# Dilated attention: the table for the exchange of weights is made one unit earlier on VectorE

## The chip, the cores and the metric

The kernel runs on one core of a Trainium2 chip. The core has five engines that work beside each other: TensorE (PE in the profile; PEld is its loading of weights), VectorE (DVE), ScalarE (ACT), GpSimd (POOL) and SyncE (SP), which issues the transfers. Each engine takes its instructions in the order written; engines wait for each other by semaphores. The metric is the device time of one execution in microseconds (us); less is better.

## The reference, cut to what matters

The program computes three transformer layers over 512 tokens of width 1024. The second layer is a dilated attention with 8 heads of width 128 in three groups (windows 128, 512 and 2048, dilations 1, 4 and 16). Each group has its own queries; keys and values are shared.

```python
def _dilated_mixer(x, w_in, w_out, pos):
    z = x @ w_in
    ...
    for g, (span, dilation) in enumerate(DIL_PAIRS):
        o, l = _dilated_window_branch(q[:, g], k, v, span, dilation)   # softmax within a band; l is its log-sum-exp
        outs.append(o)
        lses.append(l)
    wts = jax.nn.softmax(jnp.stack(lses, axis=0), axis=0).astype(v.dtype)
    o = jnp.einsum('gbht,gbhtd->bhtd', wts, jnp.stack(outs, axis=0))
```

So every token of every head needs the log-sum-exp of all the groups before the weighted probabilities can be formed. In the kernel the first group has its tokens in order of time, the others in order of their residue modulo 4; the log-sum-exps have to change places between the two orders. This is the exchange.

## The kernel before, in words

The projection `z = x @ w_in` and the attention run together. The projection is cut into 40 **units** (class `Product`, tag `c_`), five for each head: three of queries (r = 0, 1, 2), one of keys (r = 3), one of values (r = 4). A unit is 24 matmuls of 128x512 on TensorE (lines 954 to 956: high weights with high and low inputs, low weights with high inputs, for 8 tiles k).

`Chain` writes the order of each engine out by hand. For unit j:

- TensorE (`Chain.pe`): the 24 matmuls; between the fourth and the fifth tile k the attention's `middle(j)`; after the last its `pe(j)`.
- ScalarE (`Chain.act`): waits until TensorE has used unit j, makes the high half of the weights of the unit four ahead (L853), copies the unit's result out of its bank (L2206), then the attention's `act(j)`.
- VectorE (`Chain.dve`): the same wait, the low half of these weights (L860, which waits for L853), the rotation of queries or keys (L2218 to L2223, not for r = 4), then the attention's `dve(j)`.

The attention (class `Dilated`) does its steps by their distance `rel` from the unit in which the values of head h are projected: `heads_at(j, (rel,))` gives the head for which unit j has this distance. The steps of one head around the change:

- rel 0 to 3: TensorE `score` (L2291, L2292, L2297, L2298) behind the unit, VectorE the row maxima (L2428 to L2431), ScalarE the exponentials (L2409) with their sums. Behind the exponentials of rel 3 ScalarE takes the logarithm of the sums (L2414, semaphore `logged`).
- rel 4: VectorE waits for `logged`, subtracts the negated maxima (L2435), spreads the eight numbers of a row over the table `flat` of 128x256 (L2440, semaphore `spread`) and adds two parts of the probabilities (L2443, semaphore `summed`). TensorE turns the values of head h behind the unit (`values`, L2310), ScalarE copies them out (L2392).
- rel 5, in the middle of the unit: TensorE waits for `spread` and does the `exchange` (L2320, L2321), then the second turn of the values (L2310), which needs the bank that ScalarE emptied with L2392. After the unit ScalarE and VectorE make the factors (L2448, L2380, L2450, L2452) and scale the probabilities (L2455 to L2459).
- rel 6 to 9: the probabilities are turned (L2330) and multiplied with the values (L2343, L2349); VectorE finishes a head with L2462 at rel 9.

Rel 5 of head h is rel 0 of head h + 1: behind the middle of that unit stands the first `score` of the next head, which waits for the rotation of its keys (L2223, done by VectorE at rel 4 of head h).

For the last head rel 1 to 9 fall behind the projection, among the matmuls of the output projection (L983, L984, L991); there VectorE has nothing between the steps of rel 3 and rel 4.

Of the kernel before, what the change touches and what calls it, by code (L numbers as in the profile page):

```python
# [273 lines left out]
class Evac:  # L274
# [8 lines left out]
    def start(self, dve):  # L283
        pass
# [4 lines left out]
    def dve(self, dve, core, b, i):  # L289
        pass  # L290
# [12 lines left out]
class Scaled(Evac):  # L303
# [5 lines left out]
    def dve(self, dve, core, b, i):  # L309
        dve.wait_ge(self.rms.late.inv, 2)  # L310
        dve.scalar_tensor_tensor(self.Z[:, b + self.off, :], core.bank(i), self.scale, core.line[INV2][:],
                                 ALU.mult, ALU.mult).then_inc(core.freed(i), 1)
# [1913 lines left out]
class Dilated:  # L2226
# [192 lines left out]
    def dve(self, dve, j):  # L2419
        core, s = self.core, self.s  # L2420
        for h, r in self.heads_at(j, (0, 1, 2, 3)):
            bank = core.psum[(3, 7)[r % 2]]
            negmax = self.stat(h, "negmax")
            dve.wait_ge(s.scored, 4 * h + r + 1)
            if h >= 2 and r == 0:
                dve.wait_ge(s.turned, 3 * h - 3)
            if r == 0:
                dve.tensor_reduce(negmax[:, 0:1], bank[:, 0:P], AX.X, ALU.max, negate=True).then_inc(s.negmax, 1)  # L2428
                dve.tensor_reduce(negmax[:, 1:2], bank[:, 2 * P:4 * P], AX.X, ALU.max, negate=True).then_inc(s.negmax, 1)
            else:  # L2430
                dve.tensor_reduce(negmax[:, 2 * r:2 * r + 2], bank.rearrange("p (e k) -> p e k", e=2), AX.X, ALU.max, negate=True).then_inc(s.negmax, 1)  # L2431
        for h, _ in self.heads_at(j, (4,)):
            negmax, lse = (self.stat(h, n) for n in ("negmax", "lse"))
            dve.wait_ge(s.logged, h + 1)
            dve.tensor_tensor(lse, lse, negmax, ALU.subtract).then_inc(s.lse, 1)  # L2435
            dve.wait_ge(s.lse, h + 1)
            if h:
                dve.wait_ge(s.exchanged, h)
            eye = core.const("eye32").rearrange("p (o i) -> p o i", o=1).broadcast_to([P, 8, 32])
            dve.tensor_tensor(self.flat.rearrange("p (g i) -> p g i", i=32), lse.rearrange("p (g o) -> p g o", o=1).broadcast_to([P, 8, 32]),  # L2440
                              eye, ALU.mult).then_inc(s.spread, 1)
            res = self.res[h % 2].rearrange("p (c g k) -> p c g k", c=4, g=2)
            dve.tensor_tensor(res[:, :, 0, :], res[:, :, 0, :], res[:, :, 1, :], ALU.add).then_inc(s.summed, 1)  # L2443
        for h, _ in self.heads_at(j, (5,)):
            negmax, sums, other, factor = (self.stat(h, n) for n in ("negmax", "sum", "other", "factor"))
            band, res = self.band[h % 2], self.res[h % 2].rearrange("p (c g k) -> p c g k", c=4, g=2)
            dve.wait_ge(s.exchanged, h + 1)
            dve.tensor_tensor(other, core.psum[4][:, 0:8], negmax, ALU.add).then_inc(s.shifted, 1)  # L2448
            dve.wait_ge(s.other, h + 1)
            dve.tensor_tensor(other, other, sums, ALU.add).then_inc(s.total, 1)  # L2450
            dve.wait_ge(s.total, h + 1)
            dve.reciprocal(factor, other).then_inc(s.inverted, 1)  # L2452
            dve.wait_ge(s.inverted, h + 1)
            by = lambda a, b, n: factor[:, a:b].rearrange("p (g o) -> p g o", o=1).broadcast_to([P, b - a, n])
            dve.tensor_scalar(band[:, 0:P], band[:, 0:P], factor[:, 0:1], None, ALU.mult).then_inc(s.scaled, 1)  # L2455
            wide = band[:, P:7 * P].rearrange("p (g k) -> p g k", g=3)
            dve.tensor_tensor(wide, wide, by(1, 4, 2 * P), ALU.mult).then_inc(s.scaled, 1)
            dve.wait_ge(s.summed, h + 1)
            dve.tensor_tensor(res[:, :, 0, :], res[:, :, 0, :], by(4, 8, P), ALU.mult).then_inc(s.scaled, 1)  # L2459
        for h, _ in self.heads_at(j, (9,)):  # L2460
            dve.wait_ge(s.src_hi, h + 1)
            dve.tensor_tensor(self.in_time(self.xl[:, h, :]), self.result(), self.in_time(self.xh[:, h, :].bitcast(F32)),  # L2462
                              ALU.subtract).then_inc(s.src_lo, 1)
# [698 lines left out]
```

## Time and profile before

| | before |
|---|---|
| median of 3 runs | 2458.71 us (2455.76 to 2458.79) |
| the profiled execution, its own time | 2457.42 us |
| its span in the trace | 2455.6 us |
| granted TensorE clock, mean over the span | 0.941 |
| TensorE busy | 2206.9 us (90%) |
| VectorE busy | 1252.5 us (51%) |
| ScalarE busy | 842.3 us (34%) |

The dilated attention with its projection lies between about 900 and 1225 us. In the timeline a line is: start in us, duration in us, engine, line of the program, operation, out<-in, shape and count; in square brackets how long the engine had been idle before it and what released it. The durations of matmuls overlap, since they are pipelined; their pace is read from start to start. A granted clock of 1.00 is TensorE's upper level (2.4 GHz), one of 0.50 the lower (1.2 GHz).

### The profile page before, as it was taken

The page shows a single profiled execution, that of the slowest core. Times are in us where ns is not written, and L with a number is a line of the kernel's source. Part 1 is how long each engine was busy: PE and PEld are TensorE (multiplying, and loading weights), DVE is VectorE, ACT ScalarE, POOL GpSimd, SP SyncE. Part 2 cuts the span into 40 slices and gives each one's busy share as a digit, 9 for nine tenths or more (in the row PEclk, how much of TensorE's full clock was granted, in tenths as well). Part 3 has the DMA queues.
Part 4 walks back from the last instruction along what each step waited for, and adds up shares of the span by engine and source line. Part 5 has one row for each costly group of instructions (what it writes and reads, how often), then busy time and mean ns, then how long its engine had stood idle before and what let it go on. Part 6 is the DMA issues. An engine that isn't in the chain of part 4 may idle for free. (4 is left out here: it accounts for less than half of the span.)

```text
span 2455.6 us, 31441 instructions
## 1 busy us (share of the span) xinstructions
PE 2206.9 (90%) x12852; PEld 1740.7 (71%) x12852; DVE 1252.5 (51%) x1663; ACT 842.3 (34%) x1304; POOL 317.9 (13%) x302
## 2 busy tenths in 40 slices
PE   8996787899999978999989999989996668999997
PEld 6863784678887867777768788876664446878875
DVE  4644761663243366565464443466576535542543
ACT  3334322353232243434343322352224234322322
POOL 0000000200000210000030690052341103000002
PEclk9997897899999989999989999999998779999999
DMA  5210000222222212121123223222110011323222
GB/s 201 95 43 14 2 4 1 95 86 90 99 95 86 95 61 69 61 69 61 35 69 112 90 95 100 97 86 94 52 44 5 1 69 61 119 73 116 95 76 70
DMA packets 50607, 177.16 MB, mean 72 GB/s; under 512 B 5616, under 2 KB 5616, under 8 KB 50208
## 3 DMA queue, kind: packets, MB, share of 16 engines
q1 hardware_dynamic: 46944, 164.65, 20.4%
q10 hardware_dynamic: 3168, 7.60, 0.8%
q0 software_dynamic: 352, 2.90, 0.3%
q8 instruction: 102, 1.67, 0.3%
q14 instruction: 41, 0.34, 0.0%
HBM read 170.94 MB, written 4.19 MB: 71 GB/s over the span
## 5 line engine op out<-in xcount | busy, mean ns | idle before, releaser
L860 DVE TENSOR_TENSOR w_lo<-w_raw,w_hi 128x1024 fp32r<-128x1024 f32 (+1 forms) x320 | 396.1, 1239 | 838.2 <-ACT w_hi L853 837.0
L954 PE MATMUL banks<-xh,w_hi 128*128 128x512 f32 x1560 | 626.1, 401 | 4.0 <-PEq L213 3.6
L853 ACT ACTIVATE w_hi<-w_raw 128x1024 fp32r<-128x1024 f32 (+1 forms) x320 | 329.0, 1031 | 863.4 <-PE banks L956 806.5
L956 PE MATMUL banks<-xh,w_lo 128*128 128x512 f32 x1560 | 615.0, 394 | 0.0
L955 PE MATMUL banks<-xl,w_hi 128*128 128x512 f32 x1560 | 614.5, 394 | 0.0
L954 PEld LDWEIGHTS banks<-xh,w_hi 128*128 128x128 f32 x1560 | 297.6, 191 | 83.4 <-issue 16.4
L956 PEld LDWEIGHTS banks<-xh,w_lo 128*128 128x128 f32 x1560 | 296.9, 190 | 63.9
L955 PEld LDWEIGHTS banks<-xl,w_hi 128*128 128x128 f32 x1560 | 298.0, 191 | 60.4 <-issue 0.7
L954 PE MATMUL banks<-hh,w_hi 128*128 128x512 f32 x688 | 270.6, 393 | 11.8 <-DVE w_lo L860 4.8
L956 PE MATMUL banks<-hh,w_lo 128*128 128x512 f32 x688 | 269.2, 391 | 0.0
L955 PE MATMUL banks<-hl,w_hi 128*128 128x512 f32 x688 | 269.2, 391 | 0.0
L954 PEld LDWEIGHTS banks<-hh,w_hi 128*128 128x128 f32 x688 | 130.1, 189 | 41.1 <-issue 7.3
L955 PEld LDWEIGHTS banks<-hl,w_hi 128*128 128x128 f32 x688 | 130.2, 189 | 27.4 <-issue 0.5
L956 PEld LDWEIGHTS banks<-hh,w_lo 128*128 128x128 f32 x688 | 130.0, 189 | 27.4
L590 POOL TENSOR_TENSOR line<-Y 128x512 f32<-128x512 f32 x4 | 5.2, 1294 | 1046.2 <-DVE Y L573 1046.2
L983 PE MATMUL banks<-xh,w_hi 128*128 128x512 f32 x168 | 77.1, 459 | 66.3 <-DVE w_lo L860 34.1
L983 PEld LDWEIGHTS banks<-xh,w_hi 128*128 128x128 f32 x168 | 37.1, 221 | 84.2 <-DVE w_lo L860 38.6
L984 PE MATMUL banks<-xh,w_lo 128*128 128x512 f32 x168 | 74.3, 442 | 0.0
L991 PE MATMUL banks<-xl,w_hi 128*128 128x512 f32 x168 | 54.6, 429 | 1.9 <-DVE xl L727 1.9
L701 POOL TENSOR_TENSOR line<-line,line 128x512 f32<-128x512 f32 x2 | 2.6, 1288 | 406.4 <-ACT line L694 406.4
L368 DVE TENSOR_TENSOR line<-line 128x512 f32<-128x512 f32 x64 | 48.5, 757 | 0.0
L371 DVE TENSOR_TENSOR hl<-line,hh 128x512 fp32r<-128x512 f32 x64 | 47.2, 737 | 2.2
(502 smaller groups left out, 2869.9 us busy)
## 6 DMA issues: line engine op xcount, KB each, us to landing
w_raw<-in_w SPq DMA_DIRECT2D x128, 512.0 KB, 3.5
w_raw<-in_w_gu SPq DMA_DIRECT2D x44, 512.0 KB, 3.5
w_raw<-in_w_c_in SPq DMA_DIRECT2D x40, 512.0 KB, 3.4
w_raw<-in_w_ab_in SPq DMA_DIRECT2D x27, 512.0 KB, 3.5
w_raw<-in_w_in SPq DMA_DIRECT2D x25, 512.0 KB, 3.5
w_raw<-in_w_down SPq DMA_DIRECT2D x16, 384.0 KB, 3.1
w_raw<-in_w_down SPq DMA_DIRECT2D x16, 320.0 KB, 2.8
w_raw<-in_w_ab_out SPq DMA_DIRECT2D x8, 512.0 KB, 3.5
```

Of the source, the lines that this page charges most:

```text
L368: dve.tensor_tensor(sq[:], relu[:], relu[:], ALU.mult).then_inc(self.s.squared, 1)
L371: dve.tensor_tensor(self.hl[:, b, :], sq[:], self.hh[:, b, :].bitcast(F32), ALU.subtract).then_inc(self.s.hidden_lo, 1)
L590: done(gp, gp.tensor_tensor(line[SUM][:], Y[:, 0, :], Y[:, 1, :], ALU.add), s.sum)
L701: done(gp, gp.tensor_tensor(line[SSUM][:], line[SQ0][:], line[SQ1][:], ALU.add), s.ssum)
L853: act.activation(core.w_hi[u % SLOTS][:, 0:n], core.raw[u % RAW][:, 0:n], ACT.Copy).then_inc(core.hi_ready, 1)
L860: dve.tensor_tensor(lo[:, 0:n], core.raw[u % RAW][:, 0:n], hi[:, 0:n].bitcast(F32), ALU.subtract).then_inc(core.split_ready, 1)
L954: pe.matmul(bank, hi[:, w], src.xh[:, kk, :], start=kk == 0, stop=False)
L955: pe.matmul(bank, hi[:, w], src.xl[:, kk, :], start=False, stop=False)
L956: mm = pe.matmul(bank, lo[:, w], src.xh[:, kk, :], start=False, stop=last)
L983: pe.matmul(banks[i], hi[:, w], src.xh[:, k, :], start=k == 0, stop=False)
L984: pe.matmul(banks[i], lo[:, w], src.xh[:, k, :], start=False, stop=False)
L991: mm = pe.matmul(banks[i], hi[:, w], src.xl[:, k, :], start=False, stop=k == KD - 1)
```

## The change

The three VectorE instructions of rel 4 (L2435, L2440, L2443) with their two waits are moved to rel 3, behind the row maxima of the last scores of the head, which stand just before them in the same function. Nothing else is changed; no other engine's instructions are touched.

```diff
                 dve.tensor_reduce(negmax[:, 2 * r:2 * r + 2], bank.rearrange("p (e k) -> p e k", e=2), AX.X, ALU.max, negate=True).then_inc(s.negmax, 1)
-        for h, _ in self.heads_at(j, (4,)):
+        for h, _ in self.heads_at(j, (3,)):
             negmax, lse = (self.stat(h, n) for n in ("negmax", "lse"))
             dve.wait_ge(s.logged, h + 1)
             dve.tensor_tensor(lse, lse, negmax, ALU.subtract).then_inc(s.lse, 1)
```

## Rows read from the trace of the kernel before

**Rows 1.** Waits, 900 to 1215 us: who waited for whom, total, times, longest
```profile
PE banks L2320 <- DVE dil_heads L2440: 18.9, 7, 4.8
PE banks L2330 <- DVE dil_band L2457: 2.6, 2, 1.4
```

**Rows 2.** Timeline of TensorE, second head, the unit of the exchange
```profile
978.41 0.39 PE L956 MATMUL banks<-xh,w_lo 128*128 128x512 f32 x1
981.15 0.38 PE L2320 MATMUL banks<-consts,dil_heads 128*128 128x4 f32 x2 [2.35 <-DVE dil_heads L2440]
981.62 0.70 PE L2310 MATMUL banks<-consts,dil_heads 128*128 128x128 f32 x4
982.08 0.48 PE L954 MATMUL banks<-xh,w_hi 128*128 128x512 f32 x1
986.51 0.38 PE L2291 MATMUL banks<-dil_heads 128*128 128x128 f32 x2
```

**Rows 3.** Timeline of TensorE, twelve matmuls between two steps, undisturbed
```profile
972.61 0.48 PE L954 MATMUL banks<-xh,w_hi 128*128 128x512 f32 x1
972.92 0.40 PE L955 MATMUL banks<-xl,w_hi 128*128 128x512 f32 x1
...
975.43 0.60 PE L2310 MATMUL banks<-consts,dil_heads 128*128 128x128 f32 x4
```

**Rows 4.** Timeline of VectorE, second head, rel 3 and rel 4
```profile
973.32 0.67 DVE L2431 TENSOR_REDUCE dil_band<-banks 128x2 f32<-128x512 f32 x1
976.79 1.23 DVE L860 TENSOR_TENSOR w_lo<-w_raw,w_hi 128x1024 fp32r<-128x1024 f32 x1 [2.80 <-ACT w_hi L853]
...
979.88 0.68 DVE L2223 TENSOR_TENSOR dil_heads<-line,line 32x512 f32<-32x512 f32 x1
...
980.67 0.42 DVE L2440 TENSOR_TENSOR dil_heads<-dil_band,consts 128x256 f32<-128x256 f32 x1
```

**Rows 5.** Timeline of ScalarE, second head, rel 3 and rel 4
```profile
975.08 0.21 ACT L2414 ACTIVATE dil_band<-dil_band 128x8 f32<-128x8 f32 x1
975.63 1.06 ACT L853 ACTIVATE w_hi<-w_raw 128x1024 fp32r<-128x1024 f32 x1 [0.34 <-PE banks L956]
...
977.08 0.59 ACT L2392 ACTIVATE line<-banks 128x512 f32<-128x512 f32 x1
```

**Rows 6.** Timeline, last head: ScalarE, VectorE and TensorE around the table
```profile
1206.22 0.21 ACT L2414 ACTIVATE dil_band<-dil_band 128x8 f32<-128x8 f32 x1
1206.46 0.17 DVE L2435 TENSOR_TENSOR dil_band<-dil_band 128x8 f32<-128x8 f32 x1 [1.33 <-ACT dil_band L2414]
1206.66 0.42 DVE L2440 TENSOR_TENSOR dil_heads<-dil_band,consts 128x256 f32<-128x256 f32 x1
1207.01 0.68 DVE L2443 TENSOR_TENSOR dil_res<-dil_res 128x512 f32<-128x512 f32 x1
```

**Rows 7.** Timeline of all three engines, first head
```profile
933.67 0.21 ACT L2414 ACTIVATE dil_band<-dil_band 128x8 f32<-128x8 f32 x1
934.03 0.39 PE L956 MATMUL banks<-xh,w_lo 128*128 128x512 f32 x1
934.93 1.22 DVE L860 TENSOR_TENSOR w_lo<-w_raw,w_hi 128x1024 fp32r<-128x1024 f32 x1 [2.35 <-ACT w_hi L853]
935.21 0.59 ACT L2392 ACTIVATE line<-banks 128x512 f32<-128x512 f32 x1
937.99 0.68 DVE L2223 TENSOR_TENSOR dil_heads<-line,line 32x512 f32<-32x512 f32 x1
939.26 0.59 PE L2320 MATMUL banks<-consts,dil_heads 128*128 128x4 f32 x2 [4.84 <-DVE dil_heads L2440]
940.88 0.78 PE L954 MATMUL banks<-xh,w_hi 128*128 128x512 f32 x1
945.62 0.38 PE L2291 MATMUL banks<-dil_heads 128*128 128x128 f32 x2
```

**Rows 8.** Windows: us, busy of PE, PEld, DVE, ACT, POOL, granted clock, DMA share, GB/s
```profile
971.00:979.00 8.00, 7.80 (x41) 6.25 (x39) 5.16 (x8) 4.23 (x9) 0.00 (x0) 1.00 0.22 67
983.00:984.00 1.00, 1.00 (x4) 0.71 (x3) 0.00 (x0) 0.00 (x0) 0.00 (x0) 0.50 0.00 0
1198.00:1206.00 8.00, 8.00 (x59) 7.28 (x58) 1.78 (x3) 3.96 (x14) 0.00 (x0) 1.00 0.01 2
```

**Rows 9.** Timeline of TensorE, a shorter pause, in the last head
```profile
1196.04 0.55 PE L2330 MATMUL banks<-consts,dil_band 128*128 128x128 f32 x3 [1.37 <-DVE dil_band L2457]
```

**Rows 10.** Windows, same columns, a stretch of plain matmuls elsewhere in the program
```profile
600.00:660.00 60.00, 60.00 (x267) 49.67 (x266) 17.22 (x18) 11.67 (x11) 0.00 (x0) 1.00 0.30 97
```

## The prediction

> **What bounds the kernel now.** I read the waits first, then the timelines of the engines over one head, then the granted clock. In the stretch of the dilated attention TensorE is the engine that sets the pace: units follow each other without a gap, except in one place. The list of waits shows it: TensorE sat idle before the exchange, L2320, seven times for 18.9 us, until VectorE had written the table with L2440; the next one on the list, L2330 waiting for L2457, is only 2.6 us [rows 1]. No matmul of the projection waits there for weights.
>
> The timeline of the second head shows one such pause. The last matmul of the unit's first half starts at 978.41, the exchange at 981.15, 2.35 us idle [rows 2]. On VectorE the table was written at 980.67, and directly ahead of it stand the weights' low half (L860 from 976.79) and the rotation (up to L2223 at 979.88) [rows 4]. What the table needs had long been there: the logarithm L2414 ended at 975.08 + 0.21 = 975.29 [rows 5]. So the pause is VectorE's order, not its load: it was idle for 2.80 us just before L860 [rows 4].
>
> The pause has a tail. Behind it the twelve matmuls of the second half take 986.51 - 982.08 = 4.43 us from start to start [rows 2]; undisturbed, twelve take 975.43 - 972.61 = 2.82 us [rows 3]. The granted clock explains it: 1.00 before the pause, 0.50 in 983 to 984 [rows 8], that is the upper and the lower of the two levels. TensorE had been idle just before it fell. The other heads repeat this: besides the first head's pause of 4.84 us [rows 7], six of 2.33 to 2.35 us, of which rows 2 is one, each followed by a second half of 4.42 or 4.43 us.
>
> **The change part by part.**
>
> *VectorE, rel 3: a new wait.* Behind L2431 (from 973.32, ending at 973.99) VectorE now waits for `logged`. There is no circle: the logarithm waits only for exponentials whose maxima were written before. The last head shows the new order, since there nothing stands between: the logarithm ended at 1206.22 + 0.21 = 1206.43, L2435 started at 1206.46, the table was done at 1207.08 and the sum at 1207.69, that is 0.65 and 1.26 us after the logarithm [rows 6]. Put into the second head: logarithm 975.29, table 975.94, sum 976.55. What is queued behind is L860, which waits for ScalarE's L853 (975.63 + 1.06 = 976.69) and started at 976.79 [rows 4, 5]. The three instructions fit into the idle 2.80 us with 0.24 us to spare: cost nothing. If that cover were gone, say with 0.5 us of delay, L860 and the rotation would be 0.5 us later; L860 feeds a unit four ahead, and the rotation is wanted by L2291, which TensorE reaches at about 982.4 (below), against its end at 979.88 + 0.68 = 980.56: 1.8 us of room. So still nothing.
>
> *VectorE, rel 4: three instructions gone.* What follows them comes about 1.1 us earlier. TensorE doesn't wait for it: gain nothing.
>
> *TensorE, heads two to seven.* The table is there at 975.94; TensorE arrives at the exchange one matmul behind 978.41. In the stream a matmul of 128x512 takes 2.82/12 = 0.235 us from start to start [rows 3]. So the pause is worth 981.15 - 978.41 - 0.235 = 2.51 us [rows 2]. The next wait is that of the second turn, for ScalarE's L2392, which ended at 977.08 + 0.59 = 977.67 [rows 5]: ready. Then come the twelve matmuls at the pace of rows 3 if the clock doesn't fall: 4.43 - 2.82 = 1.61 us less. Together 4.12 us a head, six heads: **24.7 us**. The first score then comes at 986.51 - 4.12 = 982.39, behind the rotation (980.56). Behind that unit everything hangs on the unit's own end, and keeps its distances.
>
> *TensorE, first head.* Here the units are shorter and things come out otherwise. The logarithm ended at 933.67 + 0.21 = 933.88, so the table is done at 934.53; TensorE arrives at 934.03 + 0.235 = 934.27 and waits 0.3 us. But then the second turn has to wait for L2392, which ends at 935.21 + 0.59 = 935.80 [rows 7]: a new pause of about 0.9 us takes the place of the old. From 935.85 the turn takes 982.08 - 981.62 = 0.46 us [rows 2] and the twelve matmuls 2.82 us, so the first score comes at 939.13 in place of 945.62: **6.5 us**. The sum on VectorE ends at 933.88 + 1.26 = 935.14, L860 starts some 0.2 us later than now (934.93), and the rotation ends near 937.99 + 0.68 + 0.2 = 938.87, just ahead of the 939.13. If it came later, the gain would shrink by that much; I take 5.5 to 6.7 us.
>
> *Last head.* VectorE's order is the same before and after, as nothing stands between rel 3 and rel 4 there: 0.
>
> *The clock.* The trace doesn't show this stretch without its pauses, so the tail is bounded: at worst the clock falls as now (the 1.61 us stay), at best it never falls. I take the upper level, since it is nearest to rows of this same attention: a pause of 1.37 us [rows 9] was followed by a clock of 1.00 [rows 8], and the pauses left are 0.3 and 0.9 us, in the first head alone.
>
> *Unknown beside that.* The two small matmuls of the exchange take 981.62 - 981.15 = 0.47 us from start to start [rows 2]; at most 0.2 us of it may go, up to 1 us in all. Later stages start some 31 us earlier and can meet other moments of the clock; one tail more or less there is 1.6 us either way.
>
> **The sum.** 24.7 + 6.5 = 31.2 us. The profiled execution took 2457.42 us (its span 2455.6 and 1.8 around it); it becomes 2426.2. That execution lies 1.3 us under the median of the runs, 2458.71, so I predict **2427 us** for the median. What is late next: nothing in heads two to seven, ScalarE's L2392 in the first, and in the last head the 1.37 us before L2330, as now.
>
> **The rivals.**
>
> *The clock falls anyway* (12%). If the fall isn't the work of the pause, but of the light matmuls at this place (128x4 and the turns), the tails stay: six heads gain 2.51 us each, 15.1 us, and the first 6.5 - (945.62 - 940.88 - 2.82 = 1.92) = 4.6 us [rows 7], together 19.7: 2439 us. For it: a tail stands behind each of the seven pauses and each time the light matmuls too, so these rows don't separate the two. Against it: a stretch of the last head, right behind a pause of 1.37 us, has 59 matmuls in 8 us, most of them small ones of scores and turns, and ran at a clock of 1.00 [rows 8, 9]. The Trainium skill, "TensorE: Matmul & The Clock Gate", section "A second HAM failure mode: psum-queue depth-cycling", speaks against the change here: by it short idle spells between groups of matmuls are enough to make the clock swing between the two levels. By that rule the small pauses that are left could keep the tails. The trace of the last head, with 1.37 us of idle and no fall, doesn't bear this out for pauses of this size.
>
> *The pause isn't on the path* (4%): the stage could be held by something hidden, the transfers of weights for one, and TensorE would wait the same time elsewhere. Gain under 5 us, 2455 to 2459. Against it: no wait of the projection's matmuls for L860 in this stretch among the waits, and transfers of 67 GB/s [rows 8] where the program elsewhere moves 97 [rows 10].
>
> *Slower* (4%): without its pauses TensorE is busy throughout, and the chip could answer that with the lower level for whole heads. At the lower level the 120 matmuls of a head take 120 x 0.235 = 28 us more. The gain of 31.2 us is eaten by a bit more than one head at the lower level; with two it would be 2427 + 56 = 2483 us. Against it: 60.00 us of 60 busy at a clock of 1.00 in a plain stretch [rows 10]. The same page of the Trainium skill, section "Seeing it yourself", tells of a limit on peak current that needs three busy cores of a die; this program has one, so by the page this rival can't come. No run here shows three.
>
> **How the numbers follow.** The forecast has 80%; its own range is 2423 (all of the unknown gains, and a lower run) to 2431 (first head at 5.5, one tail more, a higher run). The range given goes on to the case in which the clock falls anyway in some or all heads: 2422 to 2440, which leaves out little more than the two rivals of 4% and the ends of the forecast. A measurement of this kernel can tell about 0.2%, 4.9 us, from no change. Faster by more: forecast and first rival, 92%. Within: 4%. Slower: 4%.
>
> **What the profile would show.** Right: the wait of L2320 for L2440 gone but for some 0.3 us in the first head; L2435 starting within 0.1 us behind L2414 in every head, ahead of L860; the L860 of rel 4 waiting still for L853; from one exchange to the next 36.8 us in place of 40.9; a clock of 1.00 throughout heads two to seven; the mean granted clock up; in the first head a new wait of L2310 for L2392 of about 0.9 us. Wrong: a fall of the clock without a pause before it (then 2439), a new wait before L2291 (rotation too late) or before L2330, or TensorE waiting for L860. The prediction falls if the period of a head shortens by clearly less than 4.1 us.

## The result and the profile after

The changed kernel takes 2425.44 us (median of 4 runs, 2422.28 to 2428.15) against 2458.3 us before (median of 4, 2455.76 to 2458.79): a ratio of 0.9868, 95% interval 0.9851 to 0.9885. It is faster by 1.3%. The forecast was 2427 us.

The profiled execution of the changed kernel took 2428.15 us; its span is 2426.3 us and its mean granted clock 0.943. TensorE's busy time fell from 2206.9 to 2194.3 us, by 12.6 us; most of it is the seven second halves that no longer run at the lower clock, 6 x 1.6 + 1.9 = 11.4 us. The other 16.7 us of the shorter span are idle time of TensorE. VectorE and ScalarE are as busy as before:

```profile
span 2426.3 us, 31441 instructions
PE 2194.3 (90%) x12852; PEld 1733.1 (71%) x12852; DVE 1253.6 (52%) x1663; ACT 842.4 (35%) x1304; POOL 319.0 (13%) x302
```

The waits of the same stretch (900 us to the end of the projection; who waited for whom, total, times, longest), to be held against [rows 1]:

```profile
DVE dil_band L2435 <- ACT dil_band L2414: 10.6, 8, 1.3
...
PE banks L2330 <- DVE dil_band L2457: 2.6, 2, 1.4
...
PE banks L2310 <- ACT line L2392: 1.0, 2, 0.6
...
PE banks L2320 <- DVE dil_heads L2440: 0.2, 1, 0.2
```

The wait of the exchange for the table fell from 18.9 us in seven heads to 0.2 us in one. In its place VectorE waits 1.33 us for the logarithm in each head, where it had been idle anyway. (The wait of L2310 stands twice in this list: 0.65 us in the first head, which is new, and 0.34 us in the last head, which was there before.)

The second head on TensorE, ScalarE and VectorE, against [rows 2 to 5]:

```profile
970.67 0.39 PE L956 MATMUL banks<-xh,w_lo 128*128 128x512 f32 x1
970.90 0.28 PE L2320 MATMUL banks<-consts,dil_heads 128*128 128x4 f32 x2
971.04 0.36 PE L2321 MATMUL banks<-consts,dil_heads 128*128 128x4 f32 x2
971.26 0.70 PE L2310 MATMUL banks<-consts,dil_heads 128*128 128x128 f32 x4
971.72 0.48 PE L954 MATMUL banks<-xh,w_hi 128*128 128x512 f32 x1
...
974.56 0.38 PE L2291 MATMUL banks<-dil_heads 128*128 128x128 f32 x2
```

```profile
967.34 0.21 ACT L2414 ACTIVATE dil_band<-dil_band 128x8 f32<-128x8 f32 x1
967.89 1.06 ACT L853 ACTIVATE w_hi<-w_raw 128x1024 fp32r<-128x1024 f32 x1 [0.34 <-PE banks L956]
```

```profile
967.58 0.17 DVE L2435 TENSOR_TENSOR dil_band<-dil_band 128x8 f32<-128x8 f32 x1 [1.33 <-ACT dil_band L2414]
967.78 0.43 DVE L2440 TENSOR_TENSOR dil_heads<-dil_band,consts 128x256 f32<-128x256 f32 x1
968.12 0.68 DVE L2443 TENSOR_TENSOR dil_res<-dil_res 128x512 f32<-128x512 f32 x1
969.06 1.23 DVE L860 TENSOR_TENSOR w_lo<-w_raw,w_hi 128x1024 fp32r<-128x1024 f32 x1 [0.25 <-ACT w_hi L853]
...
972.15 0.68 DVE L2223 TENSOR_TENSOR dil_heads<-line,line 32x512 f32<-32x512 f32 x1
```

The exchange follows the matmul ahead of it after 0.23 us: no pause. The twelve matmuls behind take 974.56 - 971.72 = 2.84 us, where they took 4.43. The table was done at 968.21, 2.7 us before it was wanted. L860 still waits 0.25 us for L853, and the rotation ends at 972.83, 1.7 us ahead of the score. The granted clock of one head, from exchange to exchange (us, busy PE, PEld, DVE, ACT, POOL, clock, DMA share, GB/s):

```profile
970.90:1007.60 36.70, 36.70 (x199) 31.06 (x198) 25.20 (x42) 16.32 (x35) 0.00 (x0) 1.00 0.23 73
```

TensorE is busy throughout and the clock stays at its upper level, though the same small matmuls still stand in the same place.

### The profile page after: what moved, and what is told of

It reads as the page before. It is cut to its first block and busy times, and to the rows that moved or that the text cites. A ratio compares the mean times of both kernels' runs of the same rounds, so it can differ in the third digit from the quotient of the medians.

```text
span 2426.3 us, 31441 instructions
## 1 busy us (share of the span) xinstructions
PE 2194.3 (90%) x12852; PEld 1733.1 (71%) x12852; DVE 1253.6 (52%) x1663; ACT 842.4 (35%) x1304; POOL 319.0 (13%) x302
## 3 DMA queue, kind: packets, MB, share of 16 engines
HBM read 170.94 MB, written 4.19 MB: 72 GB/s over the span
## 5 line engine op out<-in xcount | busy, mean ns | idle before, releaser
L860 DVE TENSOR_TENSOR w_lo<-w_raw,w_hi 128x1024 fp32r<-128x1024 f32 (+1 forms) x320 | 396.9, 1242 | 792.2 <-ACT w_hi L853 790.8
L853 ACT ACTIVATE w_hi<-w_raw 128x1024 fp32r<-128x1024 f32 (+1 forms) x320 | 329.0, 1031 | 828.8 <-PE banks L956 773.4
```

The source lines that it names most:

```text
L853: act.activation(core.w_hi[u % SLOTS][:, 0:n], core.raw[u % RAW][:, 0:n], ACT.Copy).then_inc(core.hi_ready, 1)
L860: dve.tensor_tensor(lo[:, 0:n], core.raw[u % RAW][:, 0:n], hi[:, 0:n].bitcast(F32), ALU.subtract).then_inc(core.split_ready, 1)
```

## The experiments

All kernels are edits of the one before or after. Line numbers in the program's rows shift by a few where lines were added. For each I read two things from its trace beside its time. **The stage** is the time from the first score (first L2291) to the start of the last group of L2343 in the timeline; **the rest** is what lies behind that, to the end of the span. In the kernel before the stage takes 1220.92 - 902.57 = 318.35 us and the rest 1234.7 us; in the changed kernel 1187.98 - 901.39 = 286.59 us and 1238.3 us. Kernels measured together share one **job**; a ratio is to the runs of the kernel before in the same job. An **idle reduction** is a VectorE instruction put in to take time; nobody reads its result.

**The changed kernel again.**

> The changed kernel once more, for its interval and a second profile. If the later stages' clock is what spreads its times (2422 to 2428 us), the distance from one exchange to the next is 36.7 us again and the last L2417 lies 31 to 32 us earlier, counted from the first L2291, than in the kernel before, while the end may differ by up to 6 us. If the spread comes from the dilated stage itself, that distance differs.

Measured: 2430.79 us (2430.52 to 2432.44), ratio 0.9895 (0.9880 to 0.9910). Stage 286.66 us, rest 2430.7 - 1192.14 = 1238.6 us, from exchange to exchange 36.68 us. The stage repeats to 0.1 us; what moves the total lies outside it.

**Only the table moved.**

```diff
@@ after.py, Dilated.dve, rel 3
-            res = self.res[h % 2].rearrange("p (c g k) -> p c g k", c=4, g=2)
-            dve.tensor_tensor(res[:, :, 0, :], res[:, :, 0, :], res[:, :, 1, :], ALU.add).then_inc(s.summed, 1)
+        for h, _ in self.heads_at(j, (4,)):
+            res = ...
+            dve.tensor_tensor(...).then_inc(s.summed, 1)
```

> The table (L2435, L2440) at rel 3 as in the changed kernel, the sum L2443 back at rel 4. Theory: the table alone holds TensorE, so the whole gain stays: within 1.5 us of the changed kernel (2424 to 2427), and the first head's weights' low half starts right behind the table. Rival: moving the sum out of rel 4 gave a part of the gain (it is 0.68 us in each of seven heads): then some 4 to 5 us slower than the changed kernel.

Measured: 2428.26 us (2427.50 to 2431.84), ratio 0.9886 (0.9871 to 0.9901), in one job with the kernel above. Stage 286.73 us against 286.66: the sum's place is worth nothing, the table carries the whole gain. The median lies 1.3 us above the range expected and 2.5 us under the changed kernel of this job; both are within the spread of the runs.

**The pause taken away from TensorE's side.**

```diff
@@ before.py, Dilated.pe and Dilated.middle
+        for h, _ in self.heads_at(j, (5,)):
+            self.exchange(pe, h)
         for h, r in self.heads_at(j, (0, 1, 2, 3)):
             self.score(pe, h, r)
@@
         for h, _ in self.heads_at(j, (5,)):
-            self.exchange(pe, h)
             self.values(pe, h, 1)
```

> VectorE's order as in the kernel before; instead TensorE does the exchange (L2320, L2321) behind the unit of rel 5, just ahead of the next head's first score, and no longer in its middle. Theory: only that TensorE reaches the exchange before the table is ready costs time, so this takes the pause away as well: TensorE comes 2.8 us later, the table was 2.5 us late; about 30 us faster than before (2426 to 2430), clock at 1.00 through heads two to seven. Rival: the early table is what helps, by what follows it on VectorE (L2462, factors): then this gains little, under 10 us, and a new wait shows at L2448 or L2330.

Measured: 2421.08 us (2419.03 to 2423.98), ratio 0.9855 (0.9838 to 0.9871), 5 us under the range expected. VectorE's order is that of before, and the stage still takes only 287.06 us. So it was not an early table that helped, but that TensorE and the table no longer missed each other. The 9.7 us to the changed kernel in the same job do not come from the stage (287.06 against 286.66), but from the rest: 2419.7 - 1188.64 = 1231.1 us. This became a question of its own, below.

**The table step by step later.** Four kernels put the three instructions at rel 4 in the middle of the unit's other work: behind L860 (table_1st), the shuffle L2218 (table_2nd), L2219 (table_3rd) and L2221 (table_4th). Behind L2223 is the kernel before. In the last head all four leave the table where it was. A fifth has the order of before with two idle reductions ahead of the table.

```diff
@@ HeadTiles.dve, table_3rd
         dve.stream_shuffle(self.sw, z, SWAP).then_inc(self.s.swapped, 1)
         dve.tensor_tensor(laid(self.cs), laid(z), timed(core.const("ropec", rows)), ALU.mult).then_inc(self.s.turned, 1)
+        if place is not None:            # place = self.heads.at(b, 4)
+            self.heads.table(dve, place) # L2433 to L2443 of before
@@ Dilated.dve, pause_longer_2, rel 4
+            for i in range(2):
+                dve.tensor_reduce(self.band[h % 2][:, self.STATS + 48 + i:self.STATS + 49 + i], core.const("ropec"), AX.X, ALU.max)
             negmax, lse = (self.stat(h, n) for n in ("negmax", "lse"))
```

> The three instructions stay at rel 4, but stand right behind the weights' low half L860 and ahead of the rotation. Theory: the table is ready when TensorE comes (978.65 by the times of the second head), so heads two to seven gain as in the change, 24.4 us; the first head has a pause of 2.4 us left and gains about 5; the rotation ends 1.15 us later, with 0.6 us to spare: 2428 to 2430 us. Rival: rotation too late, a new pause before L2291 in each head: 2432 or more.

> As table_1st, but one instruction later (behind the shuffle L2218): TensorE's pause before the exchange should be about 0.55 us in heads two to seven (start to start beyond a matmul). Theory all-or-nothing: a pause this short leaves the clock at 1.00, the second half of the unit takes 2.8 us: about 26 us under before, 2432. Theory in proportion: each pause brings its share of the slow stretch, the second half takes about 3.2 us: 2435.

> Behind L2219: pause of about 1.2 us. All-or-nothing: if 1.2 us is short enough, as the pause of 1.37 us in the last head before was, second half 2.8 us and 2437 us; if not, second half 4.4 us and 2447. In proportion: second half 3.6 us, 2442.

> Behind L2221: pause of about 1.8 us. All-or-nothing: either second half 2.8 us and 2441, or 4.4 us and 2452. In proportion: second half 4.0 us, 2446. The size of pause at which the half jumps lies between this and a neighbour of the series.

> The kernel before with two idle reductions of 512 columns (about 0.65 us each) ahead of the table at rel 4: the pause is 1.25 us longer, about 3.75 us. Theory: VectorE's time ahead of the table goes one to one into TensorE's pause in heads one to seven, 8.8 us, and the slow stretch behind it keeps its length or grows by no more than a microsecond: 2467 to 2473. In proportion: the slow stretch costs half as much again, 2.4 us in place of 1.6, 5 us more: 2472 with a second half of 5.2 us.

Measured (pause and second half of heads two to seven; the last two columns are those of the profiled execution):

| kernel | idle before the exchange, us | twelve matmuls behind it, us | median, us | ratio, 95% | stage, us | rest, us |
|---|---|---|---|---|---|---|
| changed kernel | 0 | 2.84 in 6 of 6 | 2430.79 | 0.9895 (0.9880 to 0.9910) | 286.66 | 1238.6 |
| table_1st | 0 | 2.85 or 2.86 in 6 of 6 | 2430.74 | 0.9888 (0.9868 to 0.9908) | 290.11 | 1238.5 |
| table_2nd | 0.42 or 0.43 | 2.84 in 6 of 6 | 2434.03 | 0.9906 (0.9877 to 0.9935) | 294.32 | 1234.1 |
| table_3rd | 1.02 or 1.03 | 2.84 in 6 of 6 | 2436.75 | 0.9917 (0.9889 to 0.9946) | 298.45 | 1234.0 |
| table_4th | 1.62 or 1.63 | 2.84 in 3, 4.42 or 4.43 in 3 | 2446.25 | 0.9955 (0.9935 to 0.9974) | 308.75 | 1233.9 |
| before | 2.33 to 2.35 | 4.42 or 4.43 in 6 of 6 | 2458.71 | 1 | 318.35 | 1234.7 |
| pause_longer_2 | 3.52 or 3.53 | 4.09 to 4.14 in 3, 4.99 to 5.05 in 3 | 2469.47 | 1.0055 (1.0032 to 1.0078) | 329.80 | 1233.4 |

The medians are from three jobs; within the series the stages are the cleaner comparison. In heads two to seven of the kernels from the changed one to before the fall of the clock is all or nothing, and comes with the longer pauses: up to 1.03 us of idle it never came, at 2.34 us always, and at 1.62 us in three heads of six, with the instructions the same. Two of these six, TensorE in the kernel table_4th (its L2323 is L2320 of before, L2294 is L2291, and L2380 is the table, L2440 of before):

```profile
979.71 0.39 PE L2323 MATMUL banks<-consts,dil_heads 128*128 128x4 f32 x2 [1.62 <-DVE dil_heads L2380]
...
980.64 0.48 PE L954 MATMUL banks<-xh,w_hi 128*128 128x512 f32 x1
...
983.48 0.27 PE L2294 MATMUL banks<-dil_heads 128*128 128x128 f32 x1
```

```profile
1018.28 0.38 PE L2323 MATMUL banks<-consts,dil_heads 128*128 128x4 f32 x2 [1.62 <-DVE dil_heads L2380]
...
1019.20 0.48 PE L954 MATMUL banks<-xh,w_hi 128*128 128x512 f32 x1
...
1023.62 0.38 PE L2294 MATMUL banks<-dil_heads 128*128 128x128 f32 x2
```

and their granted clocks (columns as above):

```profile
980.00:984.00 4.00, 4.00 (x23) 3.48 (x24) 1.84 (x3) 0.33 (x1) 0.00 (x0) 1.00 0.03 10
...
1020.00:1021.00 1.00, 1.00 (x4) 0.81 (x3) 0.42 (x1) 0.00 (x0) 0.00 (x0) 0.50 0.00 0
```

The same pause of 1.62 us, once with 2.84 us behind it and the clock at 1.00, once with 4.42 us and 0.50. The theory of shares in proportion has fallen for these kernels: nothing between 2.86 and 4.42 us came in their heads two to seven. The all-or-nothing medians for table_2nd and table_3rd were 2432 and 2437, measured 2434.03 and 2436.75; that of table_4th lies between its two cases, since half of its heads fell.

The length of a pause alone doesn't decide, though. The six heads of the kernel before are no six independent trials: they follow each other at 40.87 to 40.90 us, all alike. Other kernels have pauses of the same length elsewhere. In the last head of the kernel delayed at its end (shift_end2, below) TensorE is idle for 2.42 us, and the clock stays up:

```profile
1182.89 0.55 PE L2330 MATMUL banks<-consts,dil_band 128*128 128x128 f32 x3 [2.42 <-DVE dil_band L2460]
```

```profile
1183.00:1191.00 8.00, 8.00 (x48) 6.95 (x49) 0.43 (x1) 1.69 (x3) 0.00 (x0) 1.00 0.00 0
```

So it does behind 2.28 us in the last head of load_5 (1.00 from 1190 to 1198 us). What makes the difference, the moment of the pause or the work around it, no run here separates; table_4th shows that both outcomes come with the same pause and the same work.

Of table_1st the expectation missed the first head: its pause of 2.33 us was followed by a second half of 4.41 us, so the clock fell there too, which I had left out; the stage is 3.5 us longer than in the changed kernel in place of the 1.5 us that the expected gains (24.4 + 5.3 against 24.7 + 6.5) imply. The first heads of the other three, with pauses of 2.92 to 4.17 us, had a fall as well.

In pause_longer_2 VectorE's time did go one to one into the pause (2.34 to 3.52 us idle). The slow stretch kept about its length in three heads, with a second half near 4.1 us. In the other three the clock was at 0.50 already before the pause ended (985.5 to 985.8 us, the exchange at 985.85) and stayed there until 992 us; the second half took 5.0 us, near the 5.2 of the proportional theory. The median, 2469.47, lies in the range of the first theory and doesn't tell them apart.

**How much room VectorE has.** Idle reductions of 128x512 behind the sum at rel 3 of the changed kernel, two in load_2 and five in load_5.

```diff
@@ after.py, Dilated.dve, rel 3, behind the sum
+            for i in range(2):       # 5 in load_5
+                dve.tensor_reduce(self.band[h % 2][:, self.STATS + 48 + i:self.STATS + 49 + i], core.const("ropec"), AX.X, ALU.max)
```

> The changed kernel with two idle reductions (about 0.65 us each, 1.25 us together) on VectorE behind the sum at rel 3, so that the low half of the weights and the rotation come later. Theory of the room: L860 has 0.1 to 0.25 us to spare, the rotation 1.7 us against TensorE's first score; so L860 starts 1.1 us later and no head from two to seven loses anything; the first head loses about 0.9 us (no room there): within 1.5 us of the changed kernel. Rival: a later L860 holds TensorE at once: 6 to 8 us slower.

> The same with five reductions, about 3.1 to 3.3 us. Theory: beyond the room of 1.7 us (and the 0.2 us of idle) TensorE waits before L2291 for the rotation, 1.2 to 1.4 us in each of heads two to seven, about 2.8 us in the first: 10 to 12 us slower than the changed kernel, without a fall of the clock. If a pause of this size does bring a fall, the following unit takes 1.6 us more and it is 20 us. Rival, that the idle VectorE hides it: no slower.

load_2: 2427.56 us (2425.67 to 2432.95), ratio 0.9886 (0.9865 to 0.9906), stage 287.62 us, 1.0 longer than the changed kernel; heads two to seven have no pause and take 36.68 us each; the first head has a new pause of 0.68 us before L2291. As expected. load_5: 2439.01 us (2437.62 to 2445.03), ratio 0.9932 (0.9914 to 0.9949), stage 297.68 us, 11.0 longer. TensorE in load_5 (waits, columns as above):

```profile
PE banks L2291 <- DVE dil_heads L2223: 14.2, 8, 7.0
```

7.0 of these 14.2 us are the wait at the start of the stage, which every kernel has; the other 7.2 are new, 2.45 in the first head and 0.78 or 0.79 in each of six. Behind the six no clock fell. Behind the one of 2.45 us it did, against the expectation:

```profile
939.72 0.79 PE L2291 MATMUL banks<-dil_heads 128*128 128x128 f32 x2 [2.45 <-DVE dil_heads L2223]
```

```profile
940.00:942.50 2.50, 2.50 (x9) 1.88 (x10) 1.47 (x4) 0.00 (x0) 0.00 (x0) 0.50 0.32 75
```

The sum of 10 to 12 us came out, but by luck, since its parts are others. From the first score to the second head's exchange it is 974.37 - 900.53 = 73.84 us against 970.90 - 901.39 = 69.51, 4.3 us more in place of 2.8, the fall among them. From exchange to exchange it is 37.71 or 37.75 us against 36.68, 1.05 us a head in place of 1.2 to 1.4. The 1.4 us left fall behind the seventh head's exchange.

**Where the last microseconds went.** The rest of the program, which no kernel edits, takes 1230 to 1239 us. To see whether the moment at which it starts is enough to do this, I delayed the last head by 1.3 us.

```diff
@@ after.py, Dilated.dve, rel 5
+            if h == 7:
+                for i in range(2):
+                    dve.tensor_reduce(self.band[h % 2][:, self.STATS + 48 + i:self.STATS + 49 + i], core.const("ropec"), AX.X, ALU.max)
             dve.wait_ge(s.exchanged, h + 1)
```

> The changed kernel with two idle reductions (1.3 us) on VectorE in the last head alone, ahead of L2448, for which TensorE waits there: the dilated stage ends 1.3 us later and everything behind it comes 1.3 us later. Theory of the moment: how long the later mixers take depends on where their waits meet the granted clock (in the profiles so far the rest of the program behind the last L2343 takes 1231, 1234 to 1235 or 1238 us, with no edit there), so this rest may come out 3 to 7 us shorter than the 1238.3 to 1238.6 of the changed kernel, and the median is not 1.3 us higher but anywhere from 2422 to 2432. Rival: the rest is fixed by the change to VectorE's order: 1238.5 again, and the median 1.3 us above that of the changed kernel, 2427 to 2432.

> The kernel with the exchange behind the unit once more, against the same runs of before. Theory of the moment: its dilated stage is 287.1 us again, as long as that of the changed kernel (286.6), and the 9.7 us between their medians came from behind the stage, so the median may fall anywhere from 2420 to 2431. Rival: it is better by itself: median 2419 to 2424 again and the rest behind the stage 1231 us again.

The delayed kernel: 2422.89 us (2420.56 to 2423.35), ratio 0.9850 (0.9836 to 0.9863). Its stage is 287.94 us, 1.3 longer as meant, and its rest 2421.5 - 1191.26 = 1230.2 us, 8.4 us shorter than in the second profile of the changed kernel: the rival, 1238.5 again, is out, and the rest fell by more than the 3 to 7 us expected. The exchange behind the unit, again: 2423.15 us (2418.18 to 2428.07), ratio 0.9852 (0.9834 to 0.9869), stage 287.11, rest 1231.1. That is what its rival had said: this kernel's rest repeats, as that of the changed kernel does, so the shorter rest of the first time wasn't a chance of one execution. The late mixers, 94 us counted from 652 us behind the start of the last L2343, first before, then the changed kernel, and the delayed one (columns as above):

```profile
1872.90:1966.90 94.00, 59.75 (x619) 37.10 (x619) 42.84 (x54) 29.21 (x51) 8.41 (x4) 0.76 0.00 1
```

```profile
1840.00:1934.00 94.00, 58.91 (x597) 37.70 (x596) 40.01 (x50) 28.13 (x49) 8.39 (x4) 0.68 0.00 1
```

```profile
1843.30:1937.30 94.00, 57.75 (x658) 37.96 (x658) 43.25 (x53) 27.67 (x48) 8.40 (x4) 0.76 0.00 1
```

In the same 94 us TensorE gets through 597 matmuls in the changed kernel (596 in its second profile) at a clock of 0.68, and 658 in the delayed one at 0.76. This stretch is full of small matmuls and of waits (PE is busy about 60 of 94 us), and its mean clock lies between the two levels. The difference doesn't all arise there: by the same VectorE instruction, counted from the end of the stage, the delayed kernel is 0.7 us ahead of the changed one at 480 us, 3.2 us at 640 us and 8.3 us at 700 us.

It isn't VectorE's order that fixes the rest. load_2 has the order of the changed kernel, and its rest is that of before (2425.5 - 1190.87 = 1234.7 us, and within 1.2 us of before's at every VectorE instruction in it); table_1st has another order and the rest of the changed kernel (1238.5); the exchange behind the unit has the order of before and 1231.1. What differs between these kernels is when the rest starts. That the moment does it, by where the falls of the clock meet the work, fits all of them, but is argued: no run moves the moment and nothing else, and of each kernel but two there is one profile. The medians show no loss by the delay: its ratio of 0.9850 lies under that of the changed kernel in one job (0.9895) and next to it in the other (0.9868, with intervals that overlap). What sets the pattern in a given execution stays open; the runs of one kernel differ too (2422.28 and 2428.15 us at mean clocks of 0.948 and 0.943). No run shows that the gain of the delay would outlast another edit.

## Why the prediction was right

- **The pause and its cause**: right. VectorE's order made it, and either putting the table ahead or the exchange behind takes it away.
- **Heads two to seven**: forecast 4.12 us each. Measured from exchange to exchange 1022.02 - 981.15 = 40.87 us before and 1007.58 - 970.90 = 36.68 after: 4.19 us. Its terms: the pause 2.51, the slow half 4.43 - 2.84 = 1.59, and 0.11 from the exchange itself, whose two steps take 971.26 - 970.90 = 0.36 us in place of 0.47; together 4.21, equal within the rounding. The last was named as at most 0.2. In the list of waits the forecast passed over one of 7.0 us, of the first score at the start of the stage; it is there before and after, so nothing changes by it.
- **First head**: forecast 6.5 us. From the first score to the second head's: 945.62 - 902.57 = 43.05 us before, 937.88 - 901.39 = 36.49 after, 6.56 less. The new pause before L2310 was forecast as 0.9 and is 0.65 us idle by the trace, the one before the exchange 0.3 and is 0.20.
- **Last head**: 0, right; the stage is 318.35 - 286.59 = 31.8 us shorter, the heads above make 6 x 4.19 + 6.56 = 31.7.
- **The wait put on VectorE**: free, as said; 0.25 us of room before L860 (forecast 0.24), and load_2 and load_5 show the rotation's room of 1.7 us. A third wait moved along that the text doesn't count, for the exchange of the head before (`exchanged`); it had long been met, and no wait of the table for it shows in the trace.
- **The clock**: the case taken came true. That the tail needs the pause, and that the small matmuls alone don't bring it, is shown by the changed kernel itself, and by the series. The rival in which the clock falls anyway is out. Of short idle spells that make the clock swing (the Trainium skill, "TensorE: Matmul & The Clock Gate", section "A second HAM failure mode: psum-queue depth-cycling") the trace shows nothing for pauses up to 1.03 us in this place, and agrees from 1.62 us on, where the clock did swing. The forecast's reason, that 1.37 us in the last head passed without a fall, was a weak one: in that head 2.42 us pass too.
- **The rivals of no gain and of slower**: out. A head with TensorE busy for 36.70 us of 36.70 had a clock of 1.00. It is this row that settles the second; that it "can't come" was more than its reason bore, which speaks of one limit only.
- **The term that was mis-sized**: the later stages. I allowed one tail, 1.6 us either way. The rest took 1234.7 us before and 1238.3 or 1238.6 after, a loss of 3.6 to 3.9 us, and with a delay of 1.3 us it was 1230.2. By the two profiled executions the gain was 2457.42 - 2428.15 = 29.3 us, by the medians 32.9, and in the later job 2456.23 - 2430.79 = 25.4. The median lies within the range given, but how close it came to 2427 is partly luck.

## What to carry to other kernels

Look at an engine's order for results that others wait for while their inputs have long been there: three short instructions behind an unrelated 3.7 us cost TensorE a pause in every head, and moving either end of the wait, the maker or the taker, removed it. Count the clock with the pause: here 2.3 us of idle cost 3.9 us, and shortening it to 1.0 us already saved the clock's part. How long a pause may be before the clock falls isn't one number: 1.62 us brought a fall in some heads, and 2.42 us elsewhere brought none. Where a change saves less than one half of a per cent, compare the stage that it touches in the traces, since the rest of the program, with no edit in it, took up to 8.4 us more or less here.

## What the runs showed of the hardware

At one and the same pause of 1.62 us the granted clock fell in three heads of six and stayed in three; no pause of up to 1.03 us brought a fall there, all of 2.33 to 3.53 us did; but 2.28 us (load_5) and 2.42 us (shift_end2) in the last head brought none. In heads two to seven a fall cost 1.6 us (4.42 against 2.84 us for twelve matmuls) whether the pause was 1.62 or 2.35 us, and 1.25 to 2.2 us behind pauses of 3.5 us. With a delay of 1.3 us in one place the program behind it took 8.4 us less in the profiled executions (1230.2 against 1238.6 us), with the granted clock of the late mixers at 0.76 in place of 0.68.
